# Expert blocks of 32 slots instead of 64, and the experts behind the first three taken in turns of most and fewest tokens

## The reference, cut to what matters

```python
scores = jax.nn.sigmoid((t @ w_router).astype(jnp.float32))
...                                       # the best group of 4, and in it the best two experts
wts = jnp.take_along_axis(scores, eidx, 1)
wts = wts / jnp.sum(wts, -1, keepdims=True)
...
hid = jax.nn.silu(xblk @ w_gate[e]) * (xblk @ w_up[e])     # 1024 -> 512
return hid @ w_down[e]                                     # 512 -> 1024
...
y = jnp.zeros((n_tok + 1, d), jnp.float32).at[row_tok].add(yb.astype(jnp.float32) * row_w[:, None])
```

## Time and profile before

| | |
|---|---|
| median of 3 runs | 1379.34 us (1379.33 to 1379.9) |
| the profiled execution | 1381.63 us, its span 1379.8 us |
| PE busy | 1174.8 us, 85% of the span |
| DVE, ACT, POOL busy | 543.6, 245.6 and 192.9 us |
| DMA | 335.32 MB, mean 243 GB/s |
| mean granted TensorE clock | 0.923 |
| experts of layer 0, first gate matmul to last output | 434.86 to 740.56 us |
| experts of layer 1, the same | 1011.87 to 1326.32 us |

### The profile page before, as it was taken

The page is one execution under the profiler, slowest core; times in us unless marked ns, Lnnn a source line. Parts: engine busy times, 40 slices in busy tenths (PEclk is TensorE's granted clock), DMA queues, the critical chain, the costliest instruction groups (busy, mean ns, idle before and its releaser), DMA issues.

```text
span 1379.8 us, 18949 instructions
## 1 busy us (share of the span) xinstructions
PE 1174.8 (85%) x6946; PEld 663.1 (48%) x6947; DVE 543.6 (39%) x1319; ACT 245.6 (18%) x606; POOL 192.9 (14%) x166
## 2 busy tenths in 40 slices
PE   3999799998985999999984399989679999999940
PEld 0444344454453565666542244444445666655620
DVE  0246543462555333333322703036543333333338
ACT  0222333341120111111112111021101111111110
POOL 0011100000001111111111332300021111111123
PEclk9899999998986999999987699999779999999975
DMA  9921399982242999739995782151549996689933
GB/s 326 382 77 61 137 355 352 360 320 100 83 182 69 362 381 374 268 94 368 383 380 178 232 292 89 61 213 46 198 136 382 378 375 213 228 285 373 373 119 135
DMA packets 142758, 335.32 MB, mean 243 GB/s; under 512 B 6872, under 2 KB 9344, under 8 KB 142592
## 3 DMA queue, kind: packets, MB, share of 16 engines
q1 hardware_dynamic: 122400, 286.88, 57.1%
q0 software_dynamic: 6624, 22.55, 5.5%
q10 hardware_dynamic: 13696, 25.38, 5.4%
HBM read 315.40 MB, written 27.79 MB: 249 GB/s over the span
## 4 chain that ended last, share of the span: by engine, by line
PE 75%; DVE 9%; SPq 6%; DMA 5%; issue 2%; ACT 1%; POOL 0%; ACTq 0%; DVEq 0%; PEldq 0%; POOLq 0%
PE PS L1307 13%; PE PS L1333 11%; PE PS L1309 9%; PE PS L1240 8%; PE PS L1391 8%; PE PS L1150 7%; SPq L302 4%; PE PS L1170 3%; PE PS L1086 3%; PE PS L1270 2%; PE PS L1181 2%; DMA ring<-in_e_up_dram 2%; PE PS L1317 2%; DMA RD<-expert_rows,yidx 2%; PE PS L1275 2%
## 5 line engine op out<-in xcount | busy, mean ns | idle before, releaser
L1307 PE MATMUL PS<-ring,RE 128*64 128x256 f32 x1120 | 257.1, 389 | 22.8 <-DVE RE L973 10.3
L1309 PE MATMUL PS<-ring,RE 128*64 128x256 f32 x1120 | 257.5, 390 | 0.0
L1307 PEld LDWEIGHTS PS<-ring,RE 128*64 128x64 f32 x1120 | 155.7, 141 | 81.6 <-issue 46.0
L1001 DVE TENSOR_TENSOR RE<-RE,PS 64x256 f32<-64x256 f32 x100 | 42.3, 423 | 352.9 <-ACT RE L647 352.9
L1309 PEld LDWEIGHTS PS<-ring,RE 128*64 128x64 f32 x1120 | 155.6, 141 | 28.5 <-issue 7.0
L1333 PE MATMUL PS<-ring,RE 128*64 128x512 f32 x560 | 136.2, 602 | 0.0
L1240 PE MATMUL PS<-ring,uT 128*128 128x512 f32 x256 | 111.2, 593 | 1.9 <-ACT G L611 1.1
L1391 PE MATMUL PS<-ring,uT 128*128 128x512 f32 x256 | 110.0, 592 | 0.0
L448 POOL COPY RFW<-RE 64x1024 f32<-64x1024 f32 x50 | 52.3, 1046 | 404.4 <-PE PS L1275 390.1
L1307 PE MATMUL PS<-uT,RE 128*64 128x256 f32 x416 | 94.9, 387 | 5.0 <-DMA RD<-in_e_up_dram 4.1
L1309 PE MATMUL PS<-RD,RE 128*64 128x256 f32 x416 | 95.1, 388 | 0.0
(11 more groups left out here) (214 smaller groups left out, 1482.4 us busy)
## 6 DMA issues: line engine op xcount, KB each, us to landing
ring<-in_w_ada_dram SPq DMA_DIRECT2D x24, 2048.0 KB, 12.0
ring<-in_e_gate_dram SPq DMA_DIRECT2D x22, 2048.0 KB, 16.3
ring<-in_e_up_dram SPq DMA_DIRECT2D x22, 2048.0 KB, 19.0
ring<-in_e_down_dram SPq DMA_DIRECT2D x22, 2048.0 KB, 20.0
RD<-in_e_up_dram SPq DMA_DIRECT2D x10, 2048.0 KB, 22.8
RFW<-in_e_down_dram SPq DMA_DIRECT2D x10, 2048.0 KB, 21.7
uT<-in_e_gate_dram SPq DMA_DIRECT2D x10, 2048.0 KB, 17.1
ring<-in_b_win_dram SPq DMA_DIRECT2D x4, 2048.0 KB, 8.3
```

Source lines behind the costliest of these rows:

```text
L1001: V_.tensor_tensor(hid[:, 256 * h:256 * h + 256], gs[:, 256 * h:256 * h + 256], PS[BLK:P, h, 0:256], ALU.mult).then_inc(hid_rd[l][h], 1)
L1307: mm(PS[0:BLK, h, 0:256], xT[:, k, :], wg[:, k, 256 * h:256 * h + 256], start=(k == 0), stop=(k == DC - 1))
L1309: ins = mm(PS[BLK:P, h, 0:256], xT[:, k, :], wu[:, k, 256 * h:256 * h + 256], start=(k == 0), stop=(k == DC - 1))
```

## The change

Blocks have 32 slots (`BLK = 32`, and `CG = 4` column groups). With four column groups, gate and up of both hidden halves run side by side, and the down product is cut into four times 256 columns. Silu, multiply and transposes work on 64 partitions x 128 columns, twice a block. All indices of the layer are made at once before the loop (`ohlo`, `ohhi`, one product of 52 columns), so `onehot`, `index` and `index()` leave the loop. The gathers alternate between two buffers `xga`. The output store is four DMAs of 256 columns. The silu table is loaded once before ACT's loop and not in each pair of blocks.

The experts 3 to 15 get a new order: a rank by number of tokens (`erank`), and from it a place (`epos`), the fullest first, then the emptiest, then the second fullest, and so on. `nbp` holds the block numbers in that order, `order[l]` tells SP which expert's weights to load at each place, and `first_slot` where each expert's slots begin.

```diff
-BLK = 64
+BLK = 32
+CG = P // BLK
+    NCOL = MAXB + 4
...
-        xga = RE[0:BLK, 0:1024]
-        xg = RW[0:BLK, 1024:2048]
+        xg = RE[0:BLK, 0:1024]
+        xga = [RE[0:BLK, 2688:3712], RW[0:BLK, 1024:2048]]
```

In SP's `follow`:

```diff
+                    col = bass.ds(t * 3 + (par - 3), 1) if e is None else slice(e - 3, e - 2)
+                    src = sp.value_load(order[l][0:1, col], min_val=3, max_val=NE - 1)
                     for j in range(3):
-                        sp.wait_ge(dn_pe[l] if j == 2 else gu[l][1], last)
+                        sp.wait_ge(dn_pe[l] if j == 2 else gu[l], last)
                         sp.nop(nofuse=True)
-                        load_expert(l, t * 3 + par if e is None else e, par, j)
+                        load_expert(l, src, par, j)
```

On POOL, ahead of the loop and in it:

```diff
-                gather(0, xg, x0_in[l])
-                pool.wait_ge(ix_rd[l], 2)
-                gather(1)
+                gather(xg, x0_in[l], gidx[:, 0:1])
+                gather(xga[1], xg_in[l][1], gidx[:, 1:2])
+                gather(xga[0], xg_in[l][0], gidx[:, 2:3])
...
-                        pool.wait_ge(xg_in[l], g * 16 + 16)
+                        pool.wait_ge(xg_in[l][1 - par], gg * 16 + 16)
+                        pool.nop(nofuse=True)
+                        nc.gpsimd.tensor_copy(gcol[:, 1 - par:2 - par], gidx[:, bass.ds(g + 3, 1)]).then_inc(gc_used[l], 1)
                         pool.wait_ge(xt_pe[l], g + 1)
                         pool.nop(nofuse=True)
-                        hand_over()
-                        pool.wait_ge(ix_rd[l], g + 3)
+                        nc.gpsimd.tensor_copy(xg, xga[1 - par]).then_inc(xg_rd[l], 1)
+                        pool.wait_ge(gc_used[l], g + 1)
                         pool.nop(nofuse=True)
                         pool.wait_ge(xg_rd[l], g + 1)
                         pool.nop(nofuse=True)
-                        gather(par)
+                        gather(xga[1 - par], xg_in[l][1 - par], gcol[:, 1 - par:2 - par])
```

On ACT:

```diff
+                A(warm[:, :], ones[:, 0:1], ACT.Silu)
                 with act.Fori(0, pairs) as gg:
-                    A(warm[:, :], ones[:, 0:1], ACT.Silu)
                     for par in range(2):
                         g = gg * 2 + par
+                        act.wait_ge(gu[l], g + 1)
                         for h in range(2):
-                            act.wait_ge(gu[l][h], g + 1)
-                            A(gs[:, 256 * h:256 * h + 256], PS[0:BLK, h, 0:256], ACT.Silu).then_inc(silu_rd[l][h], 1)
+                            A(gs[:, P * h:P * h + P], PS[0:2 * BLK, 0, P * h:P * h + P], ACT.Silu).then_inc(silu_rd[l][h], 1)
+                        for h in range(2):
                             act.wait_ge(ht_pe[l][h], g + 1)
-                            A(hidT[:, 2 * h:2 * h + 2, :], PS[:, 3 + h, 0:2 * BLK].rearrange("p (k s) -> p k s", k=2),
+                            A(hidT[:, h, :, :], PS[:, 3 + h, 0:2 * BLK].rearrange("p (h s) -> p h s", h=2),
                               ACT.Copy).then_inc(ht_rd[l][h], 1)
                         act.wait_ge(y_ev[l], g + 1)
                         act.nop(nofuse=True)
-                        for q in range(2):
-                            act.dma_start(yscr[l][bass.ds(g * BLK, BLK), 512 * q:512 * q + 512],
+                        for q in range(CG):
+                            act.dma_start(yscr[l][bass.ds(g * BLK, BLK), 256 * q:256 * q + 256],
                                           ysb[par][BLK * q:BLK * q + BLK, :]).then_inc(y_st[l][par], 16)
```

On DVE, the order (the start of it; with `perm` the block numbers, the first slots and `order[l]` are then moved to their places, each with a multiply and a reduce):

```diff
+                link(V_.scalar_tensor_tensor(out=key[:, :], in0=dec16[:, 3:NE], scalar=1.0 / 32, in1=PS[:, 5, 67:80],
+                                             op0=ALU.mult, op1=ALU.add))
+                link(V_.tensor_tensor(ptmp, key[:, :].unsqueeze(1).broadcast_to([P, NF, NF]),
+                                      key[:, :].unsqueeze(2).broadcast_to([P, NF, NF]), ALU.is_gt))
+                link(V_.tensor_reduce(erank[:, :], ptmp, AX.X, ALU.add))
+                link(V_.tensor_scalar(epos[:, :], erank[:, :], -2.0, float(2 * NF - 1), ALU.mult, ALU.add))
+                link(V_.scalar_tensor_tensor(out=epos[:, :], in0=erank[:, :], scalar=2.0, in1=epos[:, :], op0=ALU.mult,
+                                             op1=ALU.min))
+                link(V_.tensor_tensor(perm, epos[:, :].unsqueeze(2).broadcast_to([P, NF, NF]),
+                                      iota_s[:, 0:NF].unsqueeze(1).broadcast_to([P, NF, NF]), ALU.is_equal))
```

On DVE, all indices at once:

```diff
+                V_.tensor_tensor(ohlo, slo[:, :, :].rearrange("p k t -> p (k t)").unsqueeze(2).broadcast_to([P, 2 * NT, BLK]),
+                                 iota_s.unsqueeze(1).broadcast_to([P, 2 * NT, BLK]), ALU.is_equal)
+                for k in range(2):
+                    for j in range(NT):
+                        ins = V_.tensor_scalar(ohhi[:, NT * k + j, :], iota_b, shi[:, k, j:j + 1], tokid[:, j:j + 1],
+                                               ALU.is_equal, ALU.mult)
+                ins.then_inc(oh_rd[l], 1)
+                dve.wait_ge(ix_pe[l], 1)
+                V_.tensor_copy(gidx[:, :], PS[0:BLK, 6, 0:NCOL]).then_inc(ix_rd[l], 1)
```

On DVE, in the loop:

```diff
-                        dve.wait_ge(xg_in[l], g * 16 + 16)
-                        dve.wait_ge(ix_pe[l], g + 4)
-                        index(1 - par)
-                        onehot(lnk)
...
-                        V_.tensor_tensor(ysb[par], PS[:, 5, :], G[:, 0:512], ALU.mult).then_inc(y_ev[l], 1)
+                        V_.tensor_tensor(ysb[par], PS[:, 5, 0:256], G[:, 0:256], ALU.mult).then_inc(y_ev[l], 1)
```

On PE, one block:

```diff
-                        for h in range(2):
-                            for k in range(DC):
-                                mm(PS[0:BLK, h, 0:256], xT[:, k, :], wg[:, k, 256 * h:256 * h + 256],
-                                   start=(k == 0), stop=(k == DC - 1))
-                                ins = mm(PS[BLK:P, h, 0:256], xT[:, k, :], wu[:, k, 256 * h:256 * h + 256],
+                        for k in range(DC):
+                            for q in range(CG):
+                                w, h = (wg, wu)[q // 2], q % 2
+                                ins = mm(PS[BLK * q:BLK * q + BLK, 0, 0:256], xT[:, k, :], w[:, k, 256 * h:256 * h + 256],
                                          start=(k == 0), stop=(k == DC - 1))
-                            ins.then_inc(gu[l][h], 1)
...
+                        ins.then_inc(gu[l], 1)
                         pe.wait_ge(xg_rd[l], g + 1)
                         pe.nop(nofuse=True)
                         turn_x()
+                        for h in range(2):
+                            pe.wait_ge(hid_rd[l][h], g + 1)
+                            pe.nop(nofuse=True)
+                            nc.tensor.transpose(PS[:, 3 + h, 0:2 * BLK], hid[:, P * h:P * h + P],
+                                                ident[0:2 * BLK, 0:2 * BLK]).then_inc(ht_pe[l][h], 1)
                         landed(2)
...
+                        for h in range(2):
                             pe.wait_ge(ht_rd[l][h], g + 1)
...
+                            for k in (h, h + 2):
+                                for q in range(CG):
+                                    ins = mm(PS[BLK * q:BLK * q + BLK, 5, 0:256], hidT[:, h, k // 2, :],
+                                             wd[:, k, 256 * q:256 * q + 256], start=(k == 0), stop=(k == FC - 1))
+                        ins.then_inc(dn_pe[l], 1)
```

More of the change, by code:

```diff
@@ L154, in backbone @@
         wsum = sb("wsum", [P, NT])
-        gtn = sb("gtn", [P, NE, NTHR])
+        gtn = RW[:, 2736:2736 + NE * NTHR].rearrange("p (e n) -> p e n", e=NE)
         gpr = sb("gpr", [P, MAXB // 2])
+        NF = NE - 3
+        key = sb("key", [P, NF])
+        erank = sb("erank", [P, NF])
+        epos = sb("epos", [P, NF])
+        perm = RW[:, 1024:1024 + NF * NF].rearrange("p (e f) -> p e f", e=NF)
+        ptmp = RW[:, 1280:1280 + NF * NF].rearrange("p (e f) -> p e f", e=NF)
+        nbp = sb("nbp", [P, NE])
+        forder = sb("forder", [P, NF])
         nbk = sb("nbk", [P, NE])
@@ L245, in backbone @@
         ix_rd = [sem(f"index_ready_{l}") for l in L]
-        xg_in = [sem(f"gathered_{l}") for l in L]
+        xg_in = [[sem(f"gathered_{l}_{b}") for b in range(2)] for l in L]
         x0_in = [sem(f"block_0_gathered_{l}") for l in L]
@@ L250, in backbone @@
         xT_rd = [sem(f"block_xT_ready_{l}") for l in L]
-        gu = [[sem(f"gate_up_{h}_in_psum_{l}") for h in range(2)] for l in L]
+        gu = [sem(f"gate_up_in_psum_{l}") for l in L]
         silu_rd = [[sem(f"silu_{h}_ready_{l}") for h in range(2)] for l in L]
@@ L411, in _ @@
             iota("thr", BLK, BLK, 0)
-            iota("pair", 2, 0, 0).then_inc(s_ic, 1)
+            iota("pair", 2, 0, 0)
+            iota("block", BLK, 0, 0).then_inc(s_ic, 1)
             pool.wait_ge(s_rope, 32)
@@ L974, in x_evac @@
                                      ALU.add).then_inc(xT_rd[l], 1)
-                onehot(link)
-                for b in range(3):
```

(18 more changed lines are left out.)

126 lines of the change are left out of this document (55 added, 71 removed).

## The result

The changed kernel takes 1339.35 us in the median (1337.26 to 1341.67, 4 runs), the kernel before 1379.62 beside it: ratio 0.971, 95% interval 0.969 to 0.972. The forecast was 1333, in the range 1306 to 1368. The profiled execution, 1337.26 with a span of 1335.5, was the fastest of the four.

What follows compares the result with a forecast made beforehand. Experts bound by PE in layer 1, by weight loads at layer 0's end. Span: 1379.8 - 45.1 (experts) + 5.8 (routing) - 7.6 (tails) = 1332.9 us; median forecast 1333, range 1306 to 1368.

Steps and rivals of the forecast that it cites:

- T: Time of one block in the experts' loop: 12.17 us before, forecast 6.85 after, bounds 6.6 to 7.1.
- the two limits: Experts' stretches: PE with 12.2 us a block and DMA weight loads with 18 us an expert, three banks between them.
- The stall of 12 in layer 0: Forecast 12 us of waiting for weight loads in layer 0's last places of two blocks, none in layer 1.
- The walk: Schedule model of blocks and weight loads in both layers' experts; forecast 289.8 and 284.7 us for the changed kernel.
- S: Least spacing between landings of an expert's weight loads: forecast 6.1 us, bounds 5.98 and 6.45.
- the routing: From `gtn` to the first gate matmul: 16.86 us before, forecast 19.8, so +5.8 over both layers.
- The tails: Last real output to first gather of outputs: layer 1 forecast 5.8 us (-6.2), layer 0 -1.4.
- Rival 1: Gate, up and down matmuls can't follow faster than 0.0625 us: T = 7.7, kernel 1390 us, slower; chance 14%.
- Rival 2: Weight loads bind more than taken: S = 6.45 gives 1347 us, 1357 with T = 7.1; chance 16%.
- Rival 3: Hand-overs inside a block overlap better: T = 6.4 and S = 5.98 give 1308 us; chance 10%.
- Rival 4: PE's clock falls because each block has two pauses of about 0.4 us: 1373 us in all; chance 3%.
- One sign of being wrong: Among the signs named against the forecast: ACT's silu in a block comes late behind its store issues.

Runs made afterwards that it cites:

- e3: Changed kernel with only the first half of each expert matrix loaded (output wrong); one execution, layer 0's experts took 282.7 us.
- e1: Changed kernel with the new order of experts 3 to 15 undone; 1377.55 us, ratio 0.999 to the kernel before.
- e2: Kernel before, with its 64-slot blocks, given only the new order of experts; 1374.08 us, ratio 0.997 to the kernel before.
- e4: Changed kernel with PE reading one loop bound per expert from the table instead of two, except a triple's first expert; 1331.5 us, ratio 0.966.
- e5: Changed kernel with gate and up of the first hidden half ahead of the second's, in rounds of 128 columns; 1336.77 us, ratio 0.970.
- e8: Changed kernel with the halves of e5, the single table read of e4 and the first half's transpose ahead of `turn_x`; 1333.92 us, ratio 0.967.
- e10: Changed kernel with each block's output stored in eight DMAs of 128 columns instead of four of 256; one execution of 1461.97 us.
- e9: The kernel of e8 with the emptiest expert first in the turns, then the fullest; 1325.08 us, ratio 0.961 to the kernel before.

## Why the prediction was right

**The block.** T was forecast at 6.85 and is 6.83, and each step of that sum holds: start of gate to silu 3.72 (forecast 3.71), silu to down product 1.39 (forecast 1.33, and 0.08 for two more waits), down product to the next gate 1.72 (forecast 1.73). Read from the chain alone they would seem to be 3.51 and 1.93, two misses that cancel; that is the 0.21 of overlap, which the chain gives to the down product.

**The places and the two limits.** 79 blocks; layer 0's last places released by loads 17.8 apart, none in layer 1: all as forecast. The stall of 12 in layer 0 is 11.0 (e3). The walk with corrected sizes gave 306 and 310 for e1 (305.6 and 311.1) and 282.3 for e3 (282.7), and with those of the kernel before 294 and 314 for e2 (295.1 and 313.1).

**The starts of experts were mis-sized.** The walk carried 0.32 and 0.9 over from the earlier trace rows; they are 0.79 and 1.30. Over ten starts and five turns that is 6.7 in layer 1, where PE is the limit. The first block's low clock cost 1.2 there and not 3, and T was 0.02 shorter over 40 blocks: 4.1 is left, and layer 1 is 4.0 longer than forecast. The mistake was to keep a price that was the exposed part of something hidden: half as many columns of down product stand in the queue when the sequencer leaves the block, and more of its 2.0 shows. e4 measured it, 5.9 in layer 1 for ten reads. In layer 0, whose end is bound by the loads, the starts are mostly absorbed in waits. Its 3.9 are more likely S: the last pieces of the loads landed 6.28 apart over eight loads (453 to 504 us) and 6.11 apart over 23 (574 to 715). An estimate by the walk, redone with the measured starts, gives 290 at S = 6.1 and 293 at 6.25, for 293.7.

**Around the loop** the routing was 19.8 in layer 0 as forecast, 18.8 in layer 1. The tails were shorter than I made them: 4.39 in layer 1 for 5.8, since the four issues took 1.6 and not 2.3 and the last store landed 1.47 after its issue and not 2.25; and 8.55 for 10.6 in layer 0.

**The sum.** 3.9 + 4.0 too little for the experts, 1.2 too much for the routing, 3.4 too much for the tails, and 0.8 less in the rest: the span came out at 1335.5 for 1332.9. That it is so near is luck in part, since these errors have both signs, and the rest holds a chance of 5.7 that had nothing to do with the change. The median is 6 above the forecast, which took it 0.5 below the profiled execution's span; it is 3.9 above. The other three executions have spans 1.7 to 4.4 longer. That they lack the early start of the profiled one is likely, but they left no trace.

**The rivals.** Rival 1, the floor of 0.0625 for a matmul, was the one to fear, with 14%. The changed kernel runs at 0.0545 and e5 at 0.027, so it is refuted; the transposes' 0.0625 was their own. The Trainium skill's figure of about 62 ns for a matmul decoded in software ("TensorE: Matmul & The Clock Gate", section "Wait — 56ns, not 53.3ns?") does not bind here; its other one, about 25 ns between starts, is just under e5's 27. Rival 2: S was 6.1 to 6.3, within the bounds. Rival 3 did not come by itself; built on purpose it gave 0.19 in e5, and in e8 T was 6.43 in a few blocks and 6.7 to 6.9 in most. Rival 4: the clock was 0.98 and 1.00 in the stretches, as it was before (0.97 and 0.99); two pauses of 0.2 a block do not lower it. With the longer pauses of e10 it fell to 0.90 and 0.89, so the rival named something that can come. One sign of being wrong did show once: in one of the 79 blocks the store issues held up ACT's silu, for 0.2.

**What the change is.** My split of the gain, 35 for the order out of 45, holds in its sense: the order undone costs 34.3 in the stretches, and alone it brings 11. Small blocks alone bring 3 (619.5 to 616.7), both changes 37 (619.5 to 582.4). The two are worth little singly and 37 together. "Small blocks" stands here for all of the change but the order, so also for the indices made ahead, the second gather buffer and the silu table ahead of the loop; none of these was undone alone. Small blocks shift the limit from PE to the loads, and only then does it matter when the loads can run.

## What to carry to other kernels

When a loop's body gets shorter, measure again what its ends cost: a table read or a branch that was free behind a long queue of work becomes a pause at each turn. Where two limits are close, write the schedule down as a walk with three or four sizes from the trace, check it on the kernel that you have, and only then judge orders and block sizes (it was right to 2 us in both layers of e1 and e2 and in layer 0 of e3, and about 10 a layer too low in e9, where the block's own time was not what it took). Packing four narrow products side by side pays at full rate, but everything that used to lie beside the wider work comes into the open. And where a change lengthens an engine's pauses, look at the granted clock of the stretch before adding up instructions.

## What the runs showed of the hardware that was not expected

Matmuls of another column group start ahead of earlier ones in the program. In the kernel with gate ahead of up, in an expert whose gate weights lie in `uT` and whose up weights in `RD`, the timeline of PE shows:
```profile
574.50 3.00 PE L1331 MATMUL PS<-uT,RE 128*32 128x256 f32 x26 [0.56 <-issue]
577.13 0.41 PE L1331 MATMUL PS<-RD,RE 128*32 128x256 f32 x2
577.31 0.41 PE L1331 MATMUL PS<-uT,RE 128*32 128x256 f32 x2
577.37 0.39 PE L1331 MATMUL PS<-RD,RE 128*32 128x256 f32 x2
577.52 0.41 PE L1331 MATMUL PS<-uT,RE 128*32 128x256 f32 x2
577.59 0.39 PE L1331 MATMUL PS<-RD,RE 128*32 128x256 f32 x2
577.74 0.41 PE L1331 MATMUL PS<-uT,RE 128*32 128x256 f32 x2
577.80 2.98 PE L1331 MATMUL PS<-RD,RE 128*32 128x256 f32 x26
```
All 32 records of `uT` stand before the first of `RD` in the program; three pairs of `RD` start while six, four and two records of `uT` are still to come. It is so in all 24 blocks with these two buffers. The four groups are busy together for three rounds, which is most of the 0.8 by which T stayed under 10.3. The Trainium skill says of matmuls that they start and end in the program's order ("TensorE: Matmul & The Clock Gate", section "The mechanism"); here the measured starts decide against it, for matmuls in different column groups.
